# Stick-breaking attention: the softplus split into a rounded part and a remainder, its suffix sums taken with rounded matmuls

## The reference, cut to what matters

```python
z = jnp.einsum('bhqd,bhkd->bhqk', qc, kT).astype(jnp.float32) * scale
valid = key_pos[None, :] < t[:, None]
sp = jnp.where(valid, jax.nn.softplus(z), 0.0)
later = lax.cumsum(sp, axis=3, reverse=True) - sp
a = jnp.where(valid, jnp.exp(jax.nn.log_sigmoid(z) - later), 0.0)
```

## Time and profile before

| | us |
|---|---|
| median of 3 runs | 1826.21 (1823.47 to 1826.26) |
| the profiled execution | 1825.83 |
| its span in the trace | 1824.0 |
| PE busy | 1732.6 (95%) |
| DVE busy | 889.3 (49%) |
| ACT busy | 751.6 (41%) |

### The profile page before, as it was taken

One profiled execution on the slowest core, in us unless ns is written; L12 is line 12 of the kernel. 1 busy time (PEld: TensorE's weight loads), 2 busy tenths in 40 slices (PEclk: granted clock), 3 DMA queues, 4 the chain that ended last, 5 costly groups with the idle time before them and its releaser, 6 DMA issues.

```text
span 1824.0 us, 26353 instructions
## 1 busy us (share of the span) xinstructions
PE 1732.6 (95%) x11036; PEld 1353.1 (74%) x11036; DVE 889.3 (49%) x1479; ACT 751.6 (41%) x1152; POOL 111.6 (6%) x117
## 2 busy tenths in 40 slices
PE   7998989989988989999999999999999999999998
PEld 6986344433444379888899988889888989988886
DVE  5485111111111165634468977536553347887743
ACT  4463112101111155644557455333565455645532
POOL 0000000000000001400200000000240020000000
PEclk9998999999999999999999999999999999999999
DMA  6344899999999925323333455535433243454552
GB/s 269 122 177 204 369 427 428 429 428 426 428 428 428 424 112 231 139 94 139 139 139 139 153 213 188 193 139 227 153 129 139 93 144 135 162 185 170 191 213 95
DMA packets 31817, 412.22 MB, mean 226 GB/s; under 512 B 3648, under 2 KB 5216, under 8 KB 6496
## 3 DMA queue, kind: packets, MB, share of 16 engines
q1 hardware_dynamic: 31712, 410.70, 57.0%
HBM read 408.85 MB, written 1.84 MB: 225 GB/s over the span
## 4 chain that ended last, share of the span: by engine, by line
PE 82%; DMA 11%; DVE 3%; ACT 2%; issue 1%; SPq 0%; POOL 0%; POOLq 0%; DVEq 0%; ACTq 0%
DMA work_mem<-in_w 9%; PE bank L1090 8%; PE bank L1239 8%; PE bank L1244 7%; PE bank L1240 7%; PE bank L1656 6%; PE bank L1275 4%; PE bank L1273 4%; PE bank L1274 4%; PE bank L1660 3%; PE bank L1113 3%; PE bank L1299 2%; PE bank L1300 2%; PE bank L1305 2%; DMA wring<-in_w 1%
## 5 line engine op out<-in xcount | busy, mean ns | idle before, releaser
L1932 ACT ACTIVATE w_hi<-wring 128x2048 fp32r<-128x2048 f32 x84 | 161.0, 1917 | 222.4 <-PE bank L1274 101.3
L2687 DVE TENSOR_TENSOR w_lo<-wring,w_hi 128x2048 fp32r<-128x2048 f32 x84 | 192.1, 2291 | 121.8 <-ACT w_hi L1932 121.7
L1932 ACT ACTIVATE w_hi_early<-wring 128x2048 fp32r<-128x2048 f32 x84 | 160.6, 1912 | 219.3 <-PE bank L1240 138.4
L1239 PE MATMUL bank<-mixed,w_hi_early 128*128 128x256 f32 x928 | 232.7, 289 | 3.5 <-DVE w_lo L2687 3.5
L1240 PE MATMUL bank<-mixed,w_hi_early 128*128 128x256 f32 x928 | 227.3, 283 | 0.0
L2687 DVE TENSOR_TENSOR w_lo<-wring,w_hi_early 128x2048 fp32r<-128x2048 f32 x84 | 191.5, 2286 | 68.0 <-ACT w_hi_early L1932 67.8
L1090 PE MATMUL bank<-wring,gates_mem 128*64 128x512 f32 x768 | 173.4, 609 | 11.6 <-DMA wring<-in_w 11.6
L1239 PEld LDWEIGHTS bank<-mixed,w_hi_early 128*128 128x128 f32 x928 | 177.5, 191 | 9.1 <-DVE w_lo L2687 4.1
L1240 PEld LDWEIGHTS bank<-mixed,w_hi_early 128*128 128x128 f32 x928 | 177.8, 192 | 0.1
L2589 DVE TENSOR_TENSOR gates_mem<-bank,gates_mem 128x512 f32<-128x512 f32 x32 | 22.1, 692 | 253.3 <-ACT gates_mem L1880 140.5
L1090 PEld LDWEIGHTS bank<-wring,gates_mem 128*64 128x64 f32 x768 | 58.3, 140 | 114.6 <-issue 114.5
(11 more groups left out here) (491 smaller groups left out, 3197.3 us busy)
## 6 DMA issues: line engine op xcount, KB each, us to landing
wring<-in_w SPq DMA_DIRECT2D x160, 2048.0 KB, 8.7
work_mem<-in_w SPq DMA_DIRECT2D x32, 2048.0 KB, 18.4
cst<-in_const SPq DMA_DIRECT2D x1, 1224.0 KB, 16.7
prm<-in_prm SPq DMA_DIRECT2D x3, 381.0 KB, 8.5
x_mem<-in_x SPq DMA_DIRECT2D x2, 512.0 KB, 4.9
out_x<-x_mem SPq DMA_DIRECT2D x2, 512.0 KB, 2.6
rel_skew<-work_mem SPq DMA_DIRECT2D x1, 768.0 KB, 3.5
work_mem<-in_prm SPq DMA_DIRECT2D x1, 512.0 KB, 16.7
```

Source lines behind the costliest of these rows:

```text
L1239: pe.matmul(out, w[0][:, k, cols], x[0][:, k, :], start=(k == 0), stop=False)
L1932: act.activation(hi, w, ACT.Copy).then_inc(hi_ready, 1)
L2687: dve.tensor_tensor(lo, w, hi, ALU.subtract).then_inc(lo_ready, 1)
```

## The change

The softplus is stored a second time as a rounded part `sp_hi` and a remainder `sp_lo`, both `fp32r`. DVE makes them for two heads at once, 768 columns, behind the second head's mask. `sp_hi` lies over `pT_s`, and `sp_lo` over `p_s` itself. The constant `sufneg` is rounded once a layer into `sufneg_r`. In the second pass the suffix sums of both key tiles are one matmul of 384 columns for each part, and the all-minus-one operand is the first column of `sufneg_r`, broadcast.

```diff
+    sp_hi, sp_lo = (view(parts(f"sp_{n}", "work_mem", first, 8 * 384), 0, 8, 384) for n, first in (("hi", 9216), ("lo", 6144)))
+    sufneg_r = parts("sufneg_r", "gates_mem", 5376, P)[:, :]
...
                 for r, j in enumerate(jobs):
-                    sp_, b = p_s[:, n + r, :], psum[j.bank]
-                    pe.matmul(b[:, S:384], C("sufneg"), sp_[:, S:384], start=False, stop=False, skip_group_check=True)
-                    pe.matmul(b[:, S:384], ident, C("negstrict"), start=False, stop=True, skip_group_check=True)
-                    pe.matmul(b[:, 0:S], C("sufneg"), sp_[:, 0:S], start=False, stop=False, skip_group_check=True)
-                    pe.matmul(b[:, P:S], negtriu[:, P:S], sp_[:, S:384], start=False, stop=False, skip_group_check=True)
+                    b, minus = psum[j.bank], sufneg_r[:, 0:1].to_broadcast([P, P])
+                    pe.matmul(b[:, S:384], ident, C("negstrict"), start=False, stop=False, skip_group_check=True)
+                    for part in (sp_hi, sp_lo):
+                        pe.matmul(b[:, 0:384], sufneg_r, part[:, n + r, :], start=False, stop=False, skip_group_check=True)
+                    for part in (sp_hi, sp_lo):
+                        pe.matmul(b[:, P:S], minus, part[:, n + r, S:384], start=False, stop=False, skip_group_check=True)
                     pe.matmul(b[:, 0:P], ident, C("negstrict"), start=False, stop=True,
                               skip_group_check=True).then_inc(bank_full[j.bank], 1)
...
                     dve.wait_ge(la_ready, l + 1)
+                    dve.tensor_copy(sufneg_r, C("sufneg"))
                     then(dve.tensor_scalar(la_m, la_m, 0.0, None, ALU.min))
...
-                    dve.tensor_tensor(corners, corners, C("strict").rearrange("p (o n) -> p o n", o=1).to_broadcast([P, 2, P]),
-                                      ALU.mult).then_inc(sb_ready, 1)
+                    ins = dve.tensor_tensor(corners, corners, C("strict").rearrange("p (o n) -> p o n", o=1).to_broadcast([P, 2, P]),
+                                            ALU.mult)
+                    if n % 2:
+                        two = slice(n - 1, n + 1)
+                        then(ins)
+                        then(dve.tensor_copy(flat2(sp_hi[:, two, :]), flat2(p_s[:, two, :])))
+                        dve.tensor_tensor(flat2(sp_lo[:, two, :]), flat2(p_s[:, two, :]), flat2(sp_hi[:, two, :]),
+                                          ALU.subtract).then_inc(sb_ready, 2)
```

## The result

| | before | after |
|---|---|---|
| median of the runs of the comparison, us | 1826.24 (8 runs, 1823.47 to 1829.16) | 1831.43 (8 runs, 1828.00 to 1833.80) |
| ratio, 95% interval | | 1.0025 [1.0013, 1.0037] |
| the profiled execution, its span, us | 1825.83, 1824.0 | 1832.79, 1830.9 |
| mean granted clock of the profiled execution | 0.982 | 0.978 |

The change makes the kernel slower by 0.25%, some 5 us. Forecast were 1826.5 us, within 1823.8 to 1830.0. Over all runs of this study the changed kernel has a mean of 1831.2 us (13 runs) and the kernel before one of 1826.3 (85 runs; two slow ones, of 4776 and 4862 us, are left out): 4.9 us are to be explained.

A forecast was written before the change was run, and what follows sets the result against it. PE was taken to bound the stage, waiting for DVE's weight split in step 0. Stage +0.18 and constant +0.15 us a layer, times two, gave +0.66 on 1825.83: 1826.5 us, range 1823.8 to 1830.0.

The forecast's parts named there:

- The stage without the clock: The changed stage in each layer: PE's savings and DVE's delays, taken step by step at full clock, come to +0.18 us.
- The waits forecast at 2.72, 0.32, 0.6 and 0 us: PE's waits for DVE's weight split in steps 0 to 3 of the stage; step 0 grows from 1.12 us.
- The split: DVE's weight splits behind every pair's scores come 1.60 us later, because the new cast and subtraction stand ahead.
- the constant: DVE's extra cast once a layer, in sparse attention, lengthens PE's wait for ACT's copy by 0.15 us.
- the shortest terms of the prediction: Lower bounds for PE's new matmuls in the second pass: 0.84 us saved a pair, 0.2 us faster in all.
- The clock: Rival: the 2.72 us wait in step 0 halves PE's clock, 2.35 us lost twice; +5.4 us, 1831.2; chance 0.08.
- two cases, 1.12 us (no fall) and 4.77 us (fall): PE idle times in the trace: granted clock 1.00 after 1.12 us, 0.50 after 4.77; 2.72 lies between.
- Short rounded matmuls dear: Rival: rounded 128-column matmuls in the second pass cost as float32; +2.4 us, 1828.2; chance 0.28 together with a slower cast.
- DVE's work hidden: Rival: DVE's new work doesn't delay the split, the step 0 wait doesn't grow; -4.3 us, 1821.5; chance 0.04.

The follow-up runs named there:

- e3: The changed kernel with DVE making the first weight split of each step ahead of the scores; 1820.41 us, ratio 0.9970.
- e4: The kernel before the change with DVE making the first weight split of each step ahead of the scores; 1821.75 us, ratio 0.9979.
- e9: e3 with 64 already met semaphore waits added on PE in layer 0's feed-forward part; 1819.18 us, ratio 0.9959.
- e2: The changed kernel with DVE's cast and subtraction behind the first weight split of the step, not ahead of it; 1821.11 us, ratio 0.9976.
- e7: PE's part of the change alone against the kernel before: softplus stored rounded, no remainder made, rounded part multiplied twice; 1821.75 us, ratio 0.9977.
- e10: The kernel before the change with one extra subtraction of 768 columns on DVE behind pair 0 alone; 1829.65 us, ratio 1.0020.
- e1: The changed kernel run once more, unaltered; ratio 1.0036 against the kernel before, profiled execution 1827.86 us.
- e5: The kernel before the change with DVE's cast and subtraction behind every pair, into scratch nothing reads; 1832.33 us, ratio 1.0029.
- e8: The changed kernel with 32 already met semaphore waits added on PE in layer 0's feed-forward part; 1833.0 us, ratio 1.0033.
- e11: The kernel before the change with one cast and one subtraction of 768 columns on DVE behind pair 0 alone; 1831.61 us, ratio 1.0032.
- e12: The changed kernel with 64 already met semaphore waits added on PE in layer 0's feed-forward part; 1829.01 us, ratio 1.0014.
- e6: The kernel before the change with DVE's cast and subtraction behind pair 0 only, both done twice; 1834.43 us, ratio 1.0044.

## Why the prediction was wrong

**The stage without the clock: right.** The waits forecast at 2.72, 0.32, 0.6 and 0 us measure 2.77, 0.16, 0.4 and 0. The split comes 1.66 us later (1.60). A layer loses 0.3 us (0.18), and the constant costs 0.15 (0.15). Twice the sum of the two is 0.9 us, against 0.66. (With the shortest terms of the prediction a pair saves 0.83 us and not its 0.84, which moves nothing.)

**What failed first: the step from the wait of 2.72 us to the sum, which left the clock at full speed.** It put at nothing what is worth about 1.9 us a run (7 falls behind 12 such waits, below). The clock was named as a rival, with 0.08. What the profiles of before, after and all experiments show behind the step-0 wait:

| wait of PE in step 0, us | kernels | falls |
|---|---|---|
| none | e3, e4, e9 | 0 of 6 |
| 1.1 to 1.2 | before, e2, e7 | 0 of 6 |
| 2.1 | e10 | 0 of 2 |
| 2.7 to 2.8 | after, e1, e5, e8, e11, e12 | 7 of 12 |
| 4.3 | e6 | 2 of 2 |

The prediction had two cases, 1.12 us (no fall) and 4.77 us (fall), and 2.72 between them. Against the fall it had only that PE is dense on either side of the wait. No row showed that this matters, and the runs speak against it: PE is as dense there in e5 and e11, and the clock falls behind 3 of 4 waits. With one case to either side, 0.08 was too low. In size the rival was wrong the other way: it took 4.7 us at half clock and 2.35 us of cost for each of two falls, where a fall is mostly 3.4 us at half clock and costs 1.4. That its 1831.2 us is what was measured is luck: 2.1 us of the measured difference have nothing to do with this wait.

**What failed too, and nobody had on the list: the start of layer 1.** The prediction followed every engine's instructions through the stage, and took the rest of the program, but for the constant, as unchanged. That put 2.1 us at nothing, 1.2 for the landing and 0.9 for falls. But 32 PE instructions fewer in layer 0 move the fetches of all that follow, and one now lies inside the 2 MB that layer 1 waits for: +1.2 us (e12, e9), and a wait of 2.3 to 2.5 us of PE behind which the clock falls too (after, e1, e2, e8; not e3, e7: 4 of 6, against 0 of 8 with 1.1 to 1.3 us). Neither failure alone takes the time out of the range of 1823.8 to 1830.0: with the fetch moved away, and the falls in step 0 left, the changed kernel measures 1829.0 us (e12), and the stage, the constant and the 2.1 us without those falls make about 1829.3.

**The account.** Stage 0.6, constant 0.3, late landing 1.2: 2.1 us without any fall, and the profiled execution of e1, which has one fall more than that of before (at 1235) and one fewer (6.8 us at half clock against 10.2 behind 1275), is 1827.86 - 1825.83 = 2.0 above it. Falls behind step 0: 7 of 12, one of them double, at 1.4 us, make 2 x 8 x 1.4 / 12 = 1.9 a run (the double one cost 2.6 and not 2.8: e8's stages of 72.7 and, in e1, 70.1). Those at the start of layer 1: two in three at 1.4 make 0.9. In all 4.9, as measured. Likewise e12: 0.9 + 1.9 = 2.8 (measured 2.4); e11: 2 x 1.6 + 1.9 = 5.1 (5.3). In others the same sum comes out higher than what was measured:

| kernel | sum against before, us | measured (means) |
|---|---|---|
| e2 | 2 x -2.35 + 0.3 + 1.2 + 0.9 = -2.3 | -4.5 |
| e3 | 2 x -3.8 + 0.3 + 1.2 + 0.9 = -5.2 | -6.1 |
| e4 | 2 x -1.4 = -2.8 | -4.4 |
| e6 | 5.5 + 4.6 = 10.1 | 8.0 |
| e7 | 2 x -2.5 + 0.3 + 1.2 + 0.9 = -2.6 | -4.2 |

e8, which should cost 4.9 us like after, costs 6.4. So the account is good to 1 or 2 us, and that it meets 4.9 to the tenth is partly luck. That each of its causes is there is shown by e2, e5, e11 and e12. The shares of the falls rest on 12 and 6 cases, so they are rough. Elsewhere falls come and go from one execution to the next in before as well: from the start of layer 1 to its stage 14 profiles read 140.0 to 143.3 us, with 3.4 to 10.2 at half clock.

**The other rivals.** Short rounded matmuls dear: false (0.06 and 0.11 us). DVE's work hidden: false as a forecast, but its price was right, since e2 and e7, which take the work off the split's way, come to 1821.1 and 1821.8 us (forecast for that case: 1821.5); but both hold the late landing of 1.2 us, which that price did not, so the agreement is partly luck. By the Trainium skill (TensorE: Matmul & The Clock Gate, section "Back-to-back issue gap") pairs sustain about 81 ns at 128 columns. The new pair of 128 columns bears that out here (0.06 and 0.11, in the mean 0.085), and the matmuls of 384 columns (0.26 and 0.18) do not match the 131 ns it gives for 512.

**What stays open.** Why 2.8 us suffice in one execution and not in the next; whether 2.1 us ever do; and the 0.9 to 2.2 us by which e2, e3, e4, e6 and e7 lie below the sum (e4: mean gain 4.4, of which its stages give 2.8). In their profiles, but for e3's, the stretch from the start of layer 1 to its stage is 1.8 to 3.2 us shorter than in that of before, with fewer microseconds at half clock; whether that holds in the mean no run shows.

## What to carry to other kernels

When an edit lengthens a wait of TensorE, price the clock too: a wait between one length that is seen to keep the clock and one that is seen to drop it deserves a real chance (here 7 of 12) and its own term in the sum, and several profiles of one kernel, since one may show the fall and the next not. Put new work of a half-idle engine behind what the bound engine waits for, not ahead of it: with its cast and subtraction ahead of the weight split the change cost 4.9 us, and with them behind it (e2) it gained 4.5. And where an edit changes the number of TensorE's instructions, look at the first large DMA behind it that something waits for, and at where the instruction fetches fall.

## What the runs showed of the hardware that was not expected

- An instruction fetch of 16 KB, by its moves TensorE's, inside a 2 MB weight DMA goes with a later landing: issue to ScalarE 8.9 to 9.1 us in six kernels with the fetch inside, 7.5 to 7.9 in the eight with it ahead of the issue. Moving it by 64 idle instructions made the landing 1.1 us (e3 to e9) and 1.3 us (after to e12) shorter, and the kernels 1.2 and, with the clock, 2.4 us faster.
- TensorE's clock fell behind 7 of 12 waits of 2.7 to 2.8 us, behind 4 of 6 of 2.3 to 2.5, and behind none of 14 of 1.1 to 1.3, each time for 3.4 us at 1.2 GHz (cost 1.4 us) or twice that (2.3 to 2.6 us: e6, e8).
- Rounded matmuls of 128 columns take 0.06 and 0.11 us in a row behind ones of 384 (0.26 and 0.18).
